# Two heads of attention as alternating matmuls on two halves of TensorE's array, and high halves of weights one tile ahead in one output product

## What is computed

```python
def context_attention(qc, kc, vc, sink):
    ...
    s = jnp.einsum('bqhgd,bkhd->bhgqk', qg, kc).astype(F32) * dh ** -0.5
    p = jax.nn.softmax(jnp.concatenate([s, _sink_column(sink, s)], axis=-1), axis=-1)
    o = jnp.einsum('bhgqk,bkhd->bqhgd', p[..., :lc].astype(vc.dtype), vc)
    return o.reshape(b, lc, ATTN_HEADS * dh)

def merge_branches(o_four, o_attn, o_hgrn, gate_raw, w_branch, w_out):
    br = jnp.stack([o_four, o_attn, o_hgrn], axis=-2)
    proj = jnp.einsum('btnc,ncd->btnd', br, w_branch)
    gates = jax.nn.sigmoid(gate_raw.reshape(gate_raw.shape[:-1] + (N_BRANCH, D_MODEL)))
    return jnp.sum(gates * proj, axis=-2) @ w_out
```

## Time and profile before

| | us |
|---|---|
| median of 3 runs | 2095.09 (2094.78 to 2096.33) |
| the profiled execution | 2094.94 |
| its span | 2093.1 |
| PE busy | 2007.8 (96% of the span) |
| PE weight loads | 1756.3 (84%) |
| DVE busy | 1267.9 (61%) |
| ACT busy | 944.5 (45%) |
| POOL busy | 433.4 (21%) |
| mean DMA rate | 143 GB/s |
| mean granted clock of PE | 0.988 of full |

### The profile page before, as it was taken

How to read it: one execution, slowest core, us unless ns; L and a number is a source line. 1 busy time by engine, 2 the same in 40 slices (tenths; PEclk the granted TensorE clock), 3 DMA queues, 4 the chain that set the end, 5 groups by cost and what they waited for, 6 DMA issues and landing times.

```text
span 2093.1 us, 30363 instructions
## 1 busy us (share of the span) xinstructions
PE 2007.8 (96%) x12246; PEld 1756.3 (84%) x12246; DVE 1267.9 (61%) x1962; ACT 944.5 (45%) x1493; POOL 433.4 (21%) x270
## 2 busy tenths in 40 slices
PE   7999899899989999999999999999989899998999
PEld 6899887899978888787688788888878898697999
DVE  5678797778855863543863583354365946776410
ACT  5444445555446333323653542243265453655643
POOL 1201000000000000000044554555500000002887
PEclk9999999999999999999999999999999999999999
DMA  7987461566722112211023344466522333144554
GB/s 254 273 295 263 159 234 41 180 223 229 264 91 95 60 48 91 91 61 61 1 81 111 109 150 143 149 202 202 181 88 94 101 121 111 51 141 142 182 191 151
DMA packets 84636, 299.22 MB, mean 143 GB/s; under 512 B 9993, under 2 KB 13201, under 8 KB 84113
## 3 DMA queue, kind: packets, MB, share of 16 engines
q1 hardware_dynamic: 64512, 231.76, 32.3%
q0 software_dynamic: 17280, 60.95, 9.1%
q10 hardware_dynamic: 2704, 4.57, 0.6%
HBM read 296.18 MB, written 4.11 MB: 143 GB/s over the span
## 4 chain that ended last, share of the span: by engine, by line
PE 79%; DVE 10%; ACT 5%; issue 3%; DMA 3%; ACTq 0%; POOL 0%; DVEq 0%; POOLq 0%
PE ps L458 21%; PE ps L453 21%; PE ps L456 21%; DVE wl L436 3%; DMA wr<-wstream 2%; ACT wh L420 2%; PE ps L1601 1%; PE ps L538 1%; PE ps L982 1%; PE ps L984 1%; PE ps L987 1%; PE ps L1042 1%; PE ps L1059 1%; PE ps L1082 1%; PE ps L1039 1%
## 5 line engine op out<-in xcount | busy, mean ns | idle before, releaser
L453 PE MATMUL ps<-HH,wh 128*128 128x256 f32 (+1 forms) x2336 | 766.8, 328 | 22.8 <-ACT HH L1320 10.7
L458 PE MATMUL ps<-HH,wl 128*128 128x256 f32 (+1 forms) x2336 | 753.5, 323 | 7.2 <-DVE wl L436 6.0
L456 PE MATMUL ps<-HL,wh 128*128 128x256 f32 (+1 forms) x2336 | 752.1, 322 | 0.5 <-DVE HL L1334 0.4
L420 ACT ACTIVATE wh<-wr 128x1024 fp32r<-128x1024 f32 x440 | 461.2, 1053 | 387.1 <-PE ps L458 333.5
L436 POOL TENSOR_TENSOR wl<-wr,wh 128x1024 fp32r<-128x1024 f32 x143 | 355.8, 2493 | 993.5 <-ACT wh L420 992.6
L436 DVE TENSOR_TENSOR wl<-wr,wh 128x1024 fp32r<-128x1024 f32 x297 | 361.8, 1227 | 246.8 <-ACT wh L420 244.4
L453 PEld LDWEIGHTS ps<-HH,wh 128*128 128x128 f32 x2336 | 449.1, 192 | 67.3 <-issue 28.7
L458 PEld LDWEIGHTS ps<-HH,wl 128*128 128x128 f32 x2336 | 448.9, 192 | 43.1 <-DVE wl L436 9.3
L456 PEld LDWEIGHTS ps<-HL,wh 128*128 128x128 f32 x2336 | 449.2, 192 | 36.9 <-issue 2.4
L458 PE MATMUL ps<-HIDH,wl 128*128 128x512 f32 (+1 forms) x512 | 173.1, 338 | 0.0
L453 PE MATMUL ps<-HIDH,wh 128*128 128x512 f32 (+1 forms) x512 | 172.8, 338 | 0.0
(11 more groups left out here) (255 smaller groups left out, 2604.1 us busy)
## 6 DMA issues: line engine op xcount, KB each, us to landing
wr<-wstream SPq DMA_DIRECT2D x440, 512.0 KB, 3.3
WM<-wmod POOLq DMA_DIRECT2D x68, 512.0 KB, 4.0
X<-wmod POOLq DMA_DIRECT2D x28, 512.0 KB, 5.4
NAB<-naskew POOLq DMA_DIRECT2D x16, 128.0 KB, 12.6
dilskew<-lines POOLq DMA_DIRECT2D x1, 2048.0 KB, 20.8
DILB<-dilskew POOLq DMA_DIRECT2D x2, 1024.0 KB, 13.5
COND<-cond ACTq DMA_DIRECT2D x2, 1024.0 KB, 5.9
CT<-consts POOLq DMA_DIRECT2D x1, 1216.0 KB, 9.5
```

Of the source, the lines that this page charges most:

```text
L420: ins = e.activation(self.WH[i % NSPL][:, :], self.WR[n % NRAW][:, :], ACT.Copy)
L453: e.matmul(out, wh, xh, start=i == 0, stop=False)
L456: e.matmul(out, wh, xl, start=False, stop=False)
L458: ins = e.matmul(out, wl, xh, start=False, stop=i == n_k - 1)
```

## The change

In each attention stage scores and values are issued for pairs of units, one on partitions 0 to 63 and one on 64 to 127, product by product in turn. The units of a layer are reordered so that the two key heads of a pair follow each other. Scores of two units are issued at odd turns, behind the transposes of unit t-2 and ahead of the filling; values of units t-3 and t-2 at odd turns behind the filling. DVE's and ACT's orders within a turn stay as they are. In the output product of layer 1, ACT makes the high halves for tile d+1 before the square of tile d, and DVE makes the low halves for tile d+1 behind the addition of tile d to X.

```diff
--- before.py
+++ after.py
@@ -257,8 +257,8 @@
 def layer_units(l):
     out = []
     for j in range(4):
-        for kv in range(2):
-            for a in range(2):
+        for a in range(2):
+            for kv in range(2):
                 out.append(Unit(("x", l, j, kv, a), "x", 1, 64 * kv, j, a, j + 4 * kv, ("xo", l, j),
                                 kv == 0 and a == 0, kv == 1 and a == 1))
     if l == 0:
@@ -1020,33 +1020,66 @@
     def unit_sink(self, u, l):
         return self.vec("attn_sink_2", 8 * l + u.head)
 
+    def score_parts(self, u):
+
+        rows, j = slice(u.off, u.off + 64), u.j
+        if u.kind == "x":
+            return [(0, 512, self.Q2[rows, j, 128 * u.a:128 * u.a + 128], self.K2[rows, :])]
+        if u.kind == "b1":
+            return [(256 * a, 256 * a + 256, self.QT[rows, j, 128 * a:128 * a + 128], self.KT[rows, j, :]) for a in range(2)]
+        return [(256 * a, 256 * a + 256, self.Q2[rows, j, 256 + 128 * a:384 + 128 * a], self.K2[rows, 256:512])
+                for a in range(2)]
+
+    def value_parts(self, u):
+
+        if u.kind == "x":
+            return [(128 * u.a, self.V2[:, c, u.off:u.off + 64], 128 * c, c == 0, c == 3) for c in range(4)]
+        if u.kind == "b1":
+            return [(128 * a, self.VR[:, k, 64 * u.head:64 * u.head + 64], 256 * a + 128 * k, k == 0, k == 1)
+                    for a in range(2) for k in range(2)]
+        return [(128 * a, self.V2[:, 2 + c, u.off:u.off + 64], 256 * a + 128 * c, c == 0, c == 1)
+                for a in range(2) for c in range(2)]
+
+    def pe_scores(self, e, w, pair, S, qk):
+
+        for u in pair:
+            S.take(u.key)
+            self.st.take(u.key)
+            self.aux.take(("s", u.key))
+            for x in self.aux.before(("s", u.key)) + qk(u):
+                w.wait_ge(*x)
+        parts = [self.score_parts(u) for u in pair]
+        for i in range(len(parts[0])):
+            for u, part in zip(pair, parts):
+                a, b, queries, keys = part[i]
+                ins = e.matmul(self.aux.item(("s", u.key))[:, a:b], queries, keys, start=True, stop=True)
+                if i == len(part) - 1:
+                    ins.then_inc(*self.c("u_score").mark(u.key))
+
+    def pe_values_of(self, e, w, pair, P, v_there):
+        group = pair[0].group
+        if pair[0].first:
+            self.main.take(group)
+            for x in self.main.before(group):
+                w.wait_ge(*x)
+        b = self.main.item(group)
+        for u in pair:
+            w.wait_ge(*self.c("u_pt").at(u.key))
+            for x in v_there(u):
+                w.wait_ge(*x)
+        parts = [self.value_parts(u) for u in pair]
+        for i in range(4):
+            for u, part in zip(pair, parts):
+                at, values, c, start, stop = part[i]
+                ins = e.matmul(b[u.off:u.off + 64, at:at + 128], values, P.item(u.key)[:, c:c + 128], start=start, stop=stop)
+                if i == 3:
+                    ins.then_inc(*self.c("u_pv").mark(u.key))
+                    P.release(u.key, self.c("u_pv"), u.key)
+
     def pe_units(self, e, w, units, rings, qk, v_there, fill):
         S, P = rings
         n = len(units)
         for t in range(-1, n + 3):
-            if t + 1 < n:
-                u = units[t + 1]
-                S.take(u.key)
-                self.st.take(u.key)
-                self.aux.take(("s", u.key))
-                b, off, j = self.aux.item(("s", u.key)), u.off, u.j
-                for x in self.aux.before(("s", u.key)):
-                    w.wait_ge(*x)
-                for x in qk(u):
-                    w.wait_ge(*x)
-                if u.kind == "b1":
-                    for a in range(2):
-                        ins = e.matmul(b[:, 256 * a:256 * a + 256], self.QT[off:off + 64, j, 128 * a:128 * a + 128],
-                                       self.KT[off:off + 64, j, :], start=True, stop=True)
-                elif u.kind == "x":
-                    ins = e.matmul(b[:, :], self.Q2[off:off + 64, j, 128 * u.a:128 * u.a + 128],
-                                   self.K2[off:off + 64, :], start=True, stop=True)
-                else:
-                    for a in range(2):
-                        ins = e.matmul(b[:, 256 * a:256 * a + 256],
-                                       self.Q2[off:off + 64, j, 256 + 128 * a:384 + 128 * a],
-                                       self.K2[off:off + 64, 256:512], start=True, stop=True)
-                ins.then_inc(*self.c("u_score").mark(u.key))
             if 2 <= t <= n + 1:
                 u = units[t - 2]
                 P.take(u.key)
@@ -1059,35 +1092,11 @@
                     ins = e.transpose(b[:, 128 * c:128 * c + 128], s[:, 128 * c:128 * c + 128], self.ident)
                 ins.then_inc(*self.c("u_tr").mark(u.key))
                 S.release(u.key, self.c("u_tr"), u.key)
+            if t % 2 and t + 1 < n:
+                self.pe_scores(e, w, units[t + 1:t + 3], S, qk)
             fill()
-            if t >= 3:
-                u = units[t - 3]
-                off, p = u.off, P.item(u.key)
-                if u.first:
-                    self.main.take(u.group)
-                    for x in self.main.before(u.group):
-                        w.wait_ge(*x)
-                b = self.main.item(u.group)
-                w.wait_ge(*self.c("u_pt").at(u.key))
-                for x in v_there(u):
-                    w.wait_ge(*x)
-                if u.kind == "b1":
-                    for a in range(2):
-                        for k in range(2):
-                            ins = e.matmul(b[off:off + 64, 128 * a:128 * a + 128],
-                                           self.VR[:, k, 64 * u.head:64 * u.head + 64],
-                                           p[:, 256 * a + 128 * k:256 * a + 128 * k + 128], start=k == 0, stop=k == 1)
-                elif u.kind == "x":
-                    for c in range(4):
-                        ins = e.matmul(b[off:off + 64, 128 * u.a:128 * u.a + 128], self.V2[:, c, off:off + 64],
-                                       p[:, 128 * c:128 * c + 128], start=c == 0, stop=c == 3)
-                else:
-                    for a in range(2):
-                        for c in range(2):
-                            ins = e.matmul(b[off:off + 64, 128 * a:128 * a + 128], self.V2[:, 2 + c, off:off + 64],
-                                           p[:, 256 * a + 128 * c:256 * a + 128 * c + 128], start=c == 0, stop=c == 1)
-                ins.then_inc(*self.c("u_pv").mark(u.key))
-                P.release(u.key, self.c("u_pv"), u.key)
+            if t % 2 and 3 <= t <= n + 1:
+                self.pe_values_of(e, w, units[t - 3:t - 1], P, v_there)
 
     def act_units(self, e, w, units, rings, l, s_free, fill):
         S, P = rings
@@ -2216,17 +2225,20 @@
     def act_add_out(self, e, w, key, ks, T, squares):
         if squares:
             self.table(e, "log_exp")
+        ahead = 1 if key == ("out", 1, 0) else 0
         for d in range(8):
-            self.make_high(e, w, *self.steps(key + (d,), ks))
+            for n in range(d + ahead if d else 0, min(d + ahead + 1, 8)):
+                self.make_high(e, w, *self.steps(key + (n,), ks))
             if squares:
                 self.act_square(e, w, key, d, self.X[:, d, 0:T], [self.c("x_new").at(key + (d, T // 256 - 1))])
 
     def dve_add_out(self, e, w, key, l, T, mod_i, squares, mod):
         w.wait_ge(*self.c("m_set").at((l, mod_i // 8)))
+        by_dve = key == ("out", 1, 0)
+        if by_dve:
+            self.make_low(e, w, "lo_dve", (key + (0,), 0))
         for d in range(8):
             k = key + (d,)
-            if key == ("out", 1, 0):
-                self.make_low(e, w, "lo_dve", (k, 0))
             if squares:
                 self.dve_square(e, w, key, d - 1, T)
             w.wait_ge(*self.c("dense").at(k))
@@ -2237,6 +2249,8 @@
                                              op0=ALU.mult, op1=ALU.add)
                 ins.then_inc(*self.c("x_new").mark(k + (c,)))
             self.main.release(k, self.c("x_new"), k + (T // 256 - 1,))
+            if by_dve and d < 7:
+                self.make_low(e, w, "lo_dve", (key + (d + 1,), 0))
             for _ in range(2 if d < 7 or key == ("ff2", 0, 0) else 0):
                 next(mod, None)
```

## The result

The changed kernel takes 2108.6 us (median; 2108.1 to 2110.2) against 2095.7 of before: ratio 1.0063 (95% interval 1.0046 to 1.0080), **12.9 us slower**. I had forecast 2096.2, and the time lies outside my range. The profiled execution has a span of 2106.3 us (before 2093.1) and a mean clock of 0.973 (before 0.988).

A forecast was written before the change was run, and what follows sets the result against it. PE was taken to bound the attention stages, DVE 15 to 27% behind, but not layer 1's output product. Output product -6.0 plus attention +7.2 gave +1.2 us: about 2096.2 us, range 2089.0 to 2103.0.

The forecast's parts named there:

- The output product: Layer 1's output product: loop per tile falls from 3.44 us to under PE's 2.80, X(7) starts earlier, -6.0 us.
- The loop of DVE: Attention stages: a serial loop through DVE sets the pair's period, 5.93 us for x units, 5.69 in block 1.
- The overlap of the halves: Attention pairs on PE: only the step to the other half shortens, to 0.05 us; a pair's values take 1.33 us.
- full overlap: Rival for attention pairs: scores and values of a pair take one unit's time; 2089.6 us in all, chance 0.25.
- my walk: All units of the attention stages stepped through three engines' orders: +7.2 us, or +0.5 with full overlap.
- my sum: The three attention stages together: block 1 -0.3, layer 0 +5.2, layer 1 +2.3, total +7.2 us.
- The gain at the heads of the stages: Head of each attention stage: dense products fill PE, so paired scores and fewer switches save about 3 us per stage.
- my short sum: Attention stages, head gain plus loop difference per pair: block 1 -0.4, layer 0 +4.3, layer 1 +1.5 us.
- The clock falls in the attention stages: Rival: PE idles more in attention, so the clock drops for a third of 200 us; +10 us, 2106, chance 0.05.
- which costs nothing: Attention pairs: PE idles 1 to 1.6 us per pair for ACT's copies, at no cost while DVE's loop is longer.

The follow-up runs named there:

- e3: The changed kernel with a pair's scores issued ahead of the transposes of the same turn; 2090.5 us, ratio 0.9984.
- e4: The changed kernel with the products of a pair issued one unit after the other instead of in turn; 2116.0 us, ratio 1.0101.
- e5: The changed kernel with an added PE product of constants, which nobody reads, in each turn from 5 on; 2098.4 us, ratio 1.0020.
- e10: The changed kernel with only the values paired; each unit's scores stand alone at the head of its turn as before; 2163.4 us, ratio 1.0323.
- e11: e10 with a pair's values moved to the end of the even turn, behind scores and transposes; 2086.8 us, ratio 0.9966.

## Why the prediction was wrong

**The output product** was right: X to X 2.80 us, X(7) 6.1 us earlier relative to the end of the attention (1900.36 - 1835.74 = 64.62; 1914.10 - 1855.56 = 58.54), -6.6 at the next product, -6 to -7 alone on the chip, against -6.0 forecast. The 0.5 us more lies behind X(7): from there to the product it is 3.97 us (1914.10 to 1918.07), where it was 4.49.

**The loop of DVE** was right: forecast 5.93 us for an x pair and 5.69 for block 1; at full clock 5.89 and 5.56. e3 shows the reason, too. (How far DVE lies behind PE I gave as 15 to 27%; in layer 0 it is 28, 62.1 of 86.0 us. Nothing hangs on it.)

**The overlap of the halves** was mis-sized. I took half a pass (1.33 us of passes for a pair's values; my own steps add up to 1.36) from the one boundary in the earlier trace rows and gave full overlap 0.25; the records show it full. The boundary in the earlier trace rows could not show more. In the kernel before the second unit's values have a wait of their own, for ACT's copy, and that copy ended at 346.34, when the first unit's eight loads (0.85 us from 345.57) were all but done:

```profile
345.57 1.90 PE L1077 MATMUL ps<-p,VR 128*64 128x128 f32 x16
345.74 0.60 ACT L1121 ACTIVATE p<-ps 128x512 f32<-128x512 f32 x1 [0.26 <-PE ps L1059]
346.39 0.85 PEld L1077 LDWEIGHTS ps<-p,VR 128*64 128x64 f32 x8
```

In the changed kernel and in e4 both waits stand ahead of the pair. By the Trainium skill, "TensorEngine Tiling (Array Packing)", section Theoretical Speedup, two halves give up to 2x: the trace agrees, with 16 records in the 1.09 us of 8. The rule of the Trainium skill, "TensorE: Matmul & The Clock Gate", Part 3, that a weight load overlaps running matmuls only where the row group differs, doesn't hold here: the two units' values use all rows and other columns, and their 16 loads take 0.88 us where 8 took 0.85. By my walk that takes 6.7 us off my sum (+0.5 instead of +7.2).

**The gain at the heads of the stages, "about -3 us in each", was not there**, and this the rows of before would have told. I counted what PE saves while dense products fill it, and walked the weight work of ACT and DVE as free-standing pieces. In truth they form a loop: DVE's low half waits for ACT's high half, which stands behind the exponential, and DVE's next reduction stands behind the low half. DVE's line 1155 in the kernel before, at the head of layer 1:

```profile
1783.77 0.41 DVE L1155 SCALAR_TENSOR_TENSOR s<-ps,CT 128x256 f32<-128x256 f32 x1
...
1788.19 0.41 DVE L1155 SCALAR_TENSOR_TENSOR s<-ps,CT 128x256 f32<-128x256 f32 x1
...
1792.61 0.41 DVE L1155 SCALAR_TENSOR_TENSOR s<-ps,CT 128x256 f32<-128x256 f32 x1
```

That is 4.42 us a unit, where the scores on PE came every 4.12: DVE and ACT were already the bound. The changed kernel has the same 4.42:

```profile
1802.43 0.41 DVE L1164 SCALAR_TENSOR_TENSOR s<-ps,CT 128x256 f32<-128x256 f32 x1
1806.85 0.41 DVE L1164 SCALAR_TENSOR_TENSOR s<-ps,CT 128x256 f32<-128x256 f32 x1
```

From the first scores of a stage to DVE's scaling of the fifth unit, block 1 takes 17.72 us before and 17.71 after, layer 0 25.11 and 24.83, layer 1 19.97 and 19.97. On PE, in e5 at a clock of 1.00, the first two pairs of layer 1 take 7.01 and 10.16 us, 17.17 together, where the four units before took 16.9; in layer 0 they take 12.18 + 9.94 = 22.1, before 21.8; in block 1 15.2, before 16.4, but there DVE's fifth unit comes no sooner for it. So the heads gave 0.3 us where my short sum had 9.0 (3.0, 3.2 and 2.8); that is more than the overlap gave. This rests on the rows; no run changed the heads alone. In e5 the stages come to +11.5 us at most by order, not +7.2.

**"The clock falls in the attention stages" was the step that decided.** I gave it 0.05, because layer 0 "already has waits for line 1176 and kept 1.00". But those waits were 0.88 us at most, and PE was busy for 56.1 of 57.0 us, 81.4 of 86.0 and 56.3 of 58.4. I had worked out myself that PE would be busy for some 60% of the loop, and that it would idle 1 to 1.6 us for ACT's copies, "which costs nothing". It idles 1.93 us in most x pairs of both layers, and the clock was 0.74 in layer 0 and 0.89 in layer 1. A wait of PE in a stage where DVE is the bound costs nothing only while the clock stays. The sum: e5 gave back 9 us (by the ratios) to 11.8 (by the stages), so the clock cost at least that; order cost 6 to 11.5. I had 0 and +7.2. What each fall of the clock follows, one long wait or many short ones, stays open. My price for the rival (+10 us) was about right; its chance was not. Its time, 2106, was the nearest to the outcome of all that I gave.

## What to carry to other kernels

Where a change takes work from PE in a stage that another engine then bounds, count the clock as a cost: here 28.7 us less of PE's busy time went with at least 9 to 12 us of loss to half clock and 6 to 11.5 to order. And look at what a row waited for before a price is taken from it: the boundary that told me "half a pass" was held by a copy. At the head of a stage, compare the period of one line on each engine to see who is the bound while the weight work runs. Of the two parts I would keep the output product alone (ratio 0.9971); no order of the attention was shown to be better.

## What the runs showed of the hardware

- Fp32 products on two halves of PE's columns or rows overlap fully when they alternate (values, column halves: 16 records in 1.09 us, 8 alone in 1.09; scores, row halves: a pair in 1.13 us, one unit in 1.12), and partly in series (values: 1.55 us) where no wait stands between the two.
- The clock can stay at its lower level for a long time although PE works most of it: 80 us at 0.50 (the 1.2 GHz level) with PE busy for 72.3 of them (e10). The Trainium skill, "TensorE: Matmul & The Clock Gate", section What's actually happening, says that activity releases the throttle. In e11 it did, some 20 us after the fall; in this stretch of e10 it did not.
- Runs of one kernel can spread with the clock: e4 from 2105.4 us at 0.985 to 2119.8 at 0.976, e5 from 2092.6 at 0.991 to 2104.5 at 0.982, before on the same chip from 2090.3 to 2096.6. The changed kernel, at 0.973 to 0.977, did not (2108.1 to 2110.2).
- The clock fell in stages whose longest wait of PE is 1.58 us (e11's layer 0), and stayed at 1.00 in those of the kernel before, whose longest is 0.88 us.
